# Expert layer: 160 instead of 128 tokens served by gathered rows, and 352 instead of 384 dense columns

## The reference, cut to what matters

```python
qh = (x2 @ w_q).reshape(t, PEER_HEADS, 2, PEER_QDIM // 2)
scores = jnp.einsum('thcd,hckd->thck', qh, sub_keys, ...)
sv, si = lax.top_k(scores, PEER_TOPK)
...
act = jax.nn.gelu(jnp.einsum('tkd,td->tk', expert_u[eb], xb, ...))
return jnp.einsum('tk,tkd->td', act * gb, expert_v[eb].astype(jnp.float32))
```

## Time and profile before

| What | Value |
|---|---|
| median of three runs | 4141.18 us (4139.8 to 4145.25) |
| the profiled execution's own time | 4136.7 us |
| its span in the trace | 4134.9 us |
| TensorE matmul busy | 3976.7 us, 96% |
| VectorE busy | 2549.7 us, 62% |
| ScalarE busy | 1551.5 us, 38% |
| GpSimd busy | 557.1 us, 13% |
| mean granted TensorE clock | 0.985 |

### The profile page before, as it was taken

The page is one execution under the profiler, slowest core; times in us unless marked ns, Lnnn a source line. Parts: engine busy times, 40 slices in busy tenths (PEclk is TensorE's granted clock), DMA queues, the critical chain, the costliest instruction groups (busy, mean ns, idle before and its releaser), DMA issues. The chain is left out here.

```text
span 4134.9 us, 50381 instructions
## 1 busy us (share of the span) xinstructions
PE 3976.7 (96%) x20625; PEld 3464.8 (84%) x20625; DVE 2549.7 (62%) x3795; ACT 1551.5 (38%) x2168; POOL 557.1 (13%) x405
## 2 busy tenths in 40 slices
PE   8999897999999899999999999999999999999998
PEld 7778797779999899999997887688888887678887
DVE  6432675679897876777776533775444442766443
ACT  3222124423666674333333224543222233744222
POOL 1000001010123333333322100100001110001000
PEclk9999999999999999999999999999999999999999
DMA  3344005333679889899983444142233434242222
GB/s 130 113 133 155 21 7 179 114 112 134 223 270 331 304 314 336 340 351 347 358 304 124 140 130 123 54 147 97 94 100 107 135 123 142 61 143 97 99 95 82
DMA packets 269057, 689.73 MB, mean 167 GB/s; under 512 B 19187, under 2 KB 52339, under 8 KB 251932
## 3 DMA queue, kind: packets, MB, share of 16 engines
q1 hardware_dynamic: 222748, 527.11, 37.1%
q0 software_dynamic: 36864, 134.23, 9.3%
q10 hardware_dynamic: 9216, 25.17, 1.5%
HBM read 585.50 MB, written 100.96 MB: 166 GB/s over the span
## 5 line engine op out<-in xcount | busy, mean ns | idle before, releaser
L1252 ACT CAST pe_w_high<-pe_w_raw 128x2048 fp32r<-128x2048 f32 (+1 forms) x168 | 317.0, 1887 | 524.3 <-DMA pe_w_raw<-in_peer_v_units 249.8
L1344 DVE TENSOR_TENSOR pe_w_low<-pe_w_raw,pe_w_high 128x2048 fp32r<-128x2048 f32 (+1 forms) x168 | 382.1, 2275 | 176.6 <-ACT pe_w_high L1252 174.7
L1139 PE MATMUL ps<-xn_p_high,pe_w_high 128*128 128x384 f32 (+1 forms) x1088 | 381.3, 350 | 34.2 <-DVE pe_w_low L1344 20.3
L2245 ACT CAST tail_w_high<-tail_w_raw 128x2048 fp32r<-128x2048 f32 (+3 forms) x124 | 221.8, 1794 | 442.5 <-DMA tail_w_raw<-in_w_in 144.3
L2254 DVE TENSOR_TENSOR tail_w_low<-tail_w_raw,tail_w_high 128x2048 fp32r<-128x2048 f32 (+3 forms) x124 | 265.7, 2147 | 186.4 <-ACT tail_w_high L2245 186.2
L1139 PE MATMUL ps<-xn_p_high,pe_w_low 128*128 128x384 f32 (+1 forms) x1088 | 371.4, 341 | 0.0
L1139 PE MATMUL ps<-xn_p_low,pe_w_high 128*128 128x384 f32 (+1 forms) x1088 | 371.2, 341 | 0.0
L1169 PE MATMUL ps<-pe_far_hidden_high,pe_w_high 128*128 128x384 f32 x1024 | 344.1, 336 | 9.3 <-DVE pe_near_hl L1470 4.7
L1169 PE MATMUL ps<-pe_near_hl,pe_w_high 128*128 128x384 f32 x1024 | 342.9, 335 | 0.0
L1169 PE MATMUL ps<-pe_far_hidden_high,pe_w_low 128*128 128x384 f32 x1024 | 342.8, 335 | 0.0
L1557 POOL DMA_INDIRECT home_pe_row<-in_peer_u,pe_expert x128 | 178.7, 1396 | 574.7 <-DVE pe_act L1530 377.6
(11 more groups left out here) (655 smaller groups left out, 9443.4 us busy)
## 6 DMA issues: line engine op xcount, KB each, us to landing
pe_w_raw<-in_peer_u_units SPq DMA_DIRECT2D x64, 1024.0 KB
pe_w_raw<-in_peer_v_units SPq DMA_DIRECT2D x64, 1024.0 KB
in_w_raw<-in_w_in SPq DMA_DIRECT2D x34, 1024.0 KB, 5.4
tail_w_raw<-in_w_up SPq DMA_DIRECT2D x32, 1024.0 KB, 5.5
tail_w_raw<-in_w_down SPq DMA_DIRECT2D x32, 1024.0 KB, 5.1
pe_w_raw<-in_w_in SPq DMA_DIRECT2D x28, 1024.0 KB
tail_w_raw<-in_w_in SPq DMA_DIRECT2D x28, 1024.0 KB, 5.1
dram_peer_hidden<-pe_rings_r ACTq DMA_DIRECT2D x64, 384.0 KB
```

The source lines that it names most:

```text
L1139: last = pe.matmul(ps[:, q, 0:n], w[:, s, at], xp[:, 4 * i + c, 0:n], start=(i == 0 and c == 0 and p == 0), stop=(i == 1 and c == 3 and p ...
L1252: act.copy(ring.flat(hi, u), ring.flat(raw, u)).then_inc(w_hi, 1)
L1344: dve.tensor_tensor(ring.flat(lo, u), ring.flat(raw, u), ring.flat(hi, u).bitcast(F32), ALU.subtract).then_inc(w_lo, 1)
L2245: act.copy(hi, raw).then_inc(self.w_hi, 1)
```

## The change

Thirty-two further tokens leave the dense way. Their 128 slots each are laid on four groups of 32 partitions (token t in group o holds slots 32o to 32o+31), so that 32 further gathers of u and 32 of v serve them: 160 + 160 gathers instead of 128 + 128. The dense way has 352 columns. The list of the 32 tokens is put on its partition groups by eight small DMAs on SyncE's queue, and their x is turned in a second tile `x_late`, four copies side by side. The last burst of gates has 32 tokens. The planner's `unit` follows from the columns (7.70 us), and sums are due from 55 us ahead of the down units instead of 5 us behind their start. The core of the diff, the repeated renamings left out:

```diff
-N_SPARSE = 128
-N_DENSE = T - N_SPARSE
-PASSES = PH * TOPK * N_SPARSE // P
+N_LATE = 32
+N_DENSE = T - P - N_LATE
+COPIES = P // N_LATE
+FIRST_PASSES = PH * TOPK
+PASSES = FIRST_PASSES + FIRST_PASSES // COPIES
...
-    GATE = lambda it: PICK[0] + 38.0 + (start(D0) - 25.0 - PICK[0] - 38.0 - 18.0 * (n_gates // 8)) / n_gates * it + 18.0 * (it // 8)
+    GATE = lambda it: PICK[0] + 38.0 + (start(D0) - 25.0 - PICK[0] - 38.0 - 18.0 * n_bursts) / n_gates * it + 18.0 * (it // 8)
...
-    first_dot, first_sum = PICK[3] + 55.0, start(D0) + 5.0
+    first_dot, first_sum = PICK[3] + 55.0, start(D0) - 55.0
+    LATE = PICK[2] + 75.0
...
                 def list_moves():
-                    if N_SPARSE < P:
-                        yield PICK[3] + 36.0
-                        sp.wait_ge(listed, 2)
-                        for t in (expert, share):
-                            sp.dma_start(t[0:N_SPARSE, 0:PASSES], t[N_SPARSE:P, PASSES:2 * PASSES]).then_inc(moved, 16)
+                    yield LATE
+                    sp.wait_ge(late_listed, 1)
+                    sp.wait_ge(ready, NT)
+                    per = FIRST_PASSES // COPIES
+                    for to, from_ in ((expert, digit), (share, ej)):
+                        rows_ = from_.rearrange("p h j -> p (h j)")
+                        for o in range(COPIES):
+                            sp.dma_start(to[o * N_LATE:(o + 1) * N_LATE, FIRST_PASSES:PASSES],
+                                         rows_[P - N_LATE:P, o * per:(o + 1) * per]).then_inc(late_moved, 16)
...
-                            parts = P // N_SPARSE
-                            for o in range(parts):
-                                last = pe.matmul(ps[:, n, N_DENSE:T], acc[:, n * P:(n + 1) * P], k.ident[:, o * N_SPARSE:(o + 1) * N_SPARSE],
-                                                 start=(o == 0), stop=(o == parts - 1))
+                            dims = slice(n * P, (n + 1) * P)
+                            for o in range(COPIES):
+                                pe.matmul(ps[:, n, N_DENSE:T - P], x_late[:, dims], k.ident[:, o * N_LATE:(o + 1) * N_LATE],
+                                          start=(o == 0), stop=(o == COPIES - 1))
+                            last = pe.matmul(ps[:, n, T - P:T], x_tok[:, dims], k.ident[:, :], start=True, stop=True)
...
+                        if m == 2:
+
+                            v(dve.tensor_scalar(digf, i1, float(NKEY), None, ALU.mult))
+                            v(dve.tensor_tensor(digf, digf, i2, ALU.add))
+                            dve.tensor_copy(digit, digf).then_inc(late_listed, 1)
...
-                            dve.tensor_tensor(to, to, by, ALU.mult).then_inc(h_scaled, 1)
...
+                            dve.tensor_tensor(to_whole, to_whole, by_whole, ALU.mult)
+                            dve.tensor_tensor(to[:, :, whole:N_DENSE], to[:, :, whole:N_DENSE], by_rest, ALU.mult).then_inc(h_scaled, 1)
...
+                    late = lambda a: a.unsqueeze(1).to_broadcast([P, COPIES, N_LATE])
+                    for c in range(NC_D):
+                        dve.scalar_tensor_tensor(x_two[1][:, c, :].rearrange("p (o t) -> p o t", o=COPIES), late(k.resid[:, c, N_DENSE:T - P]),
+                                                 gain[:, c:c + 1], late(rstd[:, N_DENSE:T - P]), ALU.mult, ALU.mult).then_inc(x_joined, 1)
...
+                            dve.wait_ge(late_moved, 32 * COPIES)
...
+                        if n == FIRST_PASSES:
+                            pool.wait_ge(late_moved, 32 * COPIES)
```

More of the change, by code:

```diff
@@ L952, in peer @@
     n_gates = N_DENSE // UNIT
+    n_bursts = -(-N_DENSE // BURST)
+    burst = lambda b: min(BURST, N_DENSE - BURST * b)
     def start(u):
@@ L992, in peer @@
     x_joined, x_turned, x_kept = sem("x_joined"), sem("x_turned"), sem("x_kept")
-    listed, moved, row_used, act_raised, folded = (sem(n) for n in ("listed", "moved", "row_used", "act_raised", "folded"))
+    late_listed, late_moved = sem("late_listed"), sem("late_moved")
+    listed, row_used, act_raised, folded = (sem(n) for n in ("listed", "row_used", "act_raised", "folded"))
     row_in = [k.gather_sem(f"{name}_row_in{s}") for s in range(DEPTH)]
@@ L1003, in peer @@
         r = rings.at("r", 0, [P, 3, 2 * N_DENSE])
[L1004 to L1007, removed]
+        x_two = [rings.at(f"x_two{i}", NC_D * P * i, [P, NC_D, P]) for i in range(2)]
+        x_tok, x_late = sb("x_tok", [P, D]), sb("x_late", [P, D])
+        of_pass = lambda j: x_tok if j < FIRST_PASSES else x_late
+        expert, share, act_s = sb("expert", [P, PASSES], U32), sb("share", [P, PASSES]), sb("act", [P, PASSES])
         rows = [k.home.at(f"{name}_row{s}", s * D, [P, D])[:, :] for s in range(DEPTH)]
@@ L1013, in peer @@
         rest = near.at("rest", 10240, [P, SETS, NKEY])
-        gate_out = near.at("gate_out", 0, [P, NKEY, BURST])
+        gate_out = [near.at(f"gate_out{t}", 0, [P, NKEY, t]) for t in (BURST, burst(n_bursts - 1))]
+        gates_of = lambda b: gate_out[0 if burst(b) == BURST else 1]
         J, I_ = ([near.at(f"{n}{s}", 8192 + 2048 * s + o, [P, UNIT, P])[:, :, :] for s in range(RING)] for n, o in (("J", 0), ("I", 1024)))
@@ L1069, in table_stores @@
                 def table_stores():
-                    for b in range(N_DENSE // BURST):
+                    for b in range(n_bursts):
                         for part in range(STORES):
-                            yield GATE(8 * b + 7) + 22.0 + unit * part
-                            sp.wait_ge(gate_kept, 16 * (b + 1))
+                            yield GATE(min(8 * b + 7, n_gates - 1)) + 22.0 + unit * part
+                            sp.wait_ge(gate_kept, min(16 * (b + 1), 2 * n_gates))
                             n = NKEY // STORES
                             quads = slice(part * n // QUAD, (part + 1) * n // QUAD)
-                            sp.dma_start(table.rearrange("u p (b x) -> p u b x", x=QUAD * BURST)[:, quads, b, :],
-                                         gate_out[:, part * n:(part + 1) * n, :].rearrange("p (u i) t -> p u (i t)", i=QUAD)
+                            columns = slice(QUAD * BURST * b, QUAD * (BURST * b + burst(b)))
+                            sp.dma_start(table.rearrange("u p x -> p u x")[:, quads, columns],
+                                         gates_of(b)[:, part * n:(part + 1) * n, :].rearrange("p (u i) t -> p u (i t)", i=QUAD)
                                          ).then_inc(gate_stored, 16)
@@ L1188, in x_turns @@
                     yield 9.0
-                    pe.wait_ge(x_joined, NC_D)
-                    for c in range(NC_D):
-                        last = pe.transpose(ps[:, 4 + c // 4, (c % 4) * P:(c % 4 + 1) * P], x_two[:, c, :], k.ident[:, :])
+                    pe.wait_ge(x_joined, 2 * NC_D)
+                    for i in range(2):
+                        for c in range(NC_D):
+                            last = pe.transpose(ps[:, 4 + 2 * i + c // 4, (c % 4) * P:(c % 4 + 1) * P], x_two[i][:, c, :], k.ident[:, :])
                     last.then_inc(x_turned, 1)
@@ L1318, in x_copies @@
                     act.wait_ge(x_turned, 1)
-                    for c in range(2):
-                        act.copy(x_tok[:, c * T:(c + 1) * T], ps[:, 4 + c, :]).then_inc(x_kept, 1)
+                    for i, to in enumerate((x_tok, x_late)):
+                        for c in range(2):
+                            act.copy(to[:, c * T:(c + 1) * T], ps[:, 4 + 2 * i + c, :]).then_inc(x_kept, 1)
                 def raise_sparse():
```

38 lines of the change are left out of this document (20 added, 18 removed).

## The result

The changed kernel takes 4164.38 us (median of 8 runs, the lowest 4151.01) beside 4145.01 us for the kernel before (8 runs): ratio 1.0042, 95% interval 1.003 to 1.0055. The change makes the kernel 0.4% slower, 19 us. I had forecast 4114 us, 27 us less than the three runs that I had then. One of the eight runs of the changed kernel took 7623 us, in a slower state; the ratio leaves it out, and the median of the other seven is 4163.55 us.

The account below looks back on a forecast made before the run. No single engine was taken as the bound: TensorE paced the down units, VectorE the choices, with DMA near full. Terms +3 + 4.5 + 12 - 23 - 22 = -26 us gave 4111 us, predicted median 4114 us, range 4078 to 4152.

Parts of the forecast that it names:

- What a unit costs TensorE: All 128 units: a matmul with 352 columns takes 0.160 us, a unit 7.67 us instead of 8.32.
- Start of the layer: Opening 106 us: eight more products and transposes ahead of TensorE's first units, +3 us.
- choices: VectorE-paced 118 us stretch: one more low half and two more dots, +4.5 us.
- the first half of the gates: 257 us stretch: added dots and low halves fill VectorE beyond the planned length, 269 us, +12.
- Second half of the gates: 304 us stretch: 104.4 MB moved at a DMA rate of 372 GB/s, 281 us, -23.
- Down units: 543 us stretch: at 372 GB/s a unit takes 8.1 us, 521 us in all, -22.
- The last unit: End of the down units: small identity products of 32 columns add 4 us.
- The sum: Whole kernel: the stretches' terms total -26 us, 4111 us profiled, 4114 us predicted for the median.
- SyncE's wait for the list: SyncE's queue: a weight load behind the wait may come late once, 0 to 10 us, taken at 0.
- the slow one: Rival: DMA engines already at their limit, 350 GB/s; kernel 21 us slower, 4163 us; chance 0.26 with its milder half.

Follow-up runs that it names:

- e2: Changed kernel with all gathers kept, but VectorE working on 8 instead of 1024 columns in every fifth slot; 4149 us, ratio 1.0012 to before.
- e1: Changed kernel with every fifth of the 320 gathers left out, VectorE's work on those slots kept; 4130 us, ratio 0.9963 to before.
- e5: Changed kernel with sums due 5 us behind the start of the down units instead of 55 us ahead; 4161 us, ratio 1.0036 to before.
- e6: Kernel before with sums due 55 us ahead of the down units, so its 128 dots are packed tighter; 4152 us, ratio 1.0014 to before.
- e8: Changed kernel with only VectorE's order in the down units altered, both low halves made earlier; 4131 us, ratio 0.9964 to before.
- e11: Changed kernel with new VectorE order in down units, sums due 5 us behind their start, SyncE's list step due 110 instead of 75 us; 4135 us.

## Why the prediction was wrong, step by step

**What a unit costs TensorE**: right, 0.159 against 0.160 us.

**Start of the layer, +3, choices, +4.5 us, and the first half of the gates, +12**: right in sign, 19.5 forecast and 25 measured. TensorE's query units end 0.3 us later, the first gate row starts at 1077.8 us instead of 1073.5, and the 192nd at 1323.9 instead of 1299.2. So the start and the choices cost 4 us instead of 7.5, and the first half 20 instead of 12. VectorE's busy time from 950 to 1325 is 347 us against 328. The reason I gave, VectorE full, is half of it: e2 shortens the up part by only 12 us. The other half is VectorE standing still for gathers, which I had not considered, though four buffers and the length of an issue were at hand.

**Second half of the gates, "104.4 / 0.372 = 281 us, -23"**: wrong. From the 192nd gate row to the down units it is 327.5 us, 330.2 before: about -3. The step took the DMA rate as what sets the length. e1, with fewer bytes, had only 10 us less up part, at 306 instead of 332 GB/s, so the rate was a result. The dots' packing, worth 12 us (e5, e6), was in my text as a formula for counting dots and not as a cost.

**Down units, "At 372 a unit takes 8.1 us ... 521 us, -22"**: wrong, 556 us, 8.7 us a unit. This is the step that turned the sign. The rate itself was well chosen: e8 reaches 365 GB/s and 517 us, within 4 us of the step's answer. What the step left out is that a rate is reached only if somebody asks in time. I wrote that the waits "eat the slack in a full queue", and never added up the chain: 10.9 us from issue to landing and 6.6 us of VectorE's order against two units of 7.67. VectorE's part of it stood in the earlier trace rows; of the landing had only the waits for it.

**The clock**: a term that is missing. With 556 us = 491 of matmuls, some 6 more of the last unit, 38 idle and up to 22 of lower clock, the down units add up. In the up part the mean of 0.95, 0.92 against 1.00, 0.98 is worth up to some 30 us. No term of my sum has the clock, though the earlier trace rows shows it.

**The last unit, 4 us**: it takes longer than that, the identity products run over 15.2 us instead of 9.1 (their first and last start):

```profile
L1187 PE MATMUL ps<-ident_sb,pe_x_late x64: 191/276/276, 2193.7 to 2208.9; 128*128 128x32 f32 x64
```

But what follows is 8 us shorter (1955 against 1963 us to the end of the span); the residual's additions overlap with the longer unit, so I take most of it as given back, without a run that shows it.

**The sum**: by the same steps the measured one is +4 (start and choices) + 20 - 3 + 14, and 8 less behind the layer: some 28 us more of span, where I had 26 less. The recorded sum has a slip of its own: 4111 + 4.5 is 4115.5 us, not 4114.

**SyncE's wait for the list**: it came (12.6 us), outside the 10 us of my bound, and cost nothing measurable (e11).

**The rivals**: the slow one named 4163 us, and 4164 was measured, but for the wrong reason. It has the DMA engines at their limit at 350 GB/s and TensorE waiting for low halves behind late loads; they ran at 338 with TensorE waiting in the down units for the low part of the hidden values alone, and gave 365 when VectorE's order was changed. The 358 GB/s of the Trainium skill's page "SBUF — State Buffer", section "Summary: rules for kernel authors", would have given the time before by the working in the prediction, and is not what held the kernel. The range's upper end, 4152, took in only half of that rival's loss; both kinds of loss that came, stalls behind VectorE and behind loads, were costs without a bound from above in my sum.

## What to carry to other kernels

Before a busy engine is made faster, add up the longest chain that must fit in its ring (issue, landing, each consumer in its fixed order) and compare it with the new length of the ring, and do the same for every other ring whose rate rises. Take late landings for this and not the median: here the median load fitted and the slower ones did not. If the chain no longer fits, the saving turns into waits, and in this kernel the longer waits also lowered TensorE's clock. The order of the instructions in a stream is then worth more than the work in it: one pair of due times gave 33 us in the changed kernel and 14 in the one before, where the whole change gave none.

## What the runs showed of the hardware that I had not expected

A matmul of 64 columns with fp32r operands, 0.213 us at a clock of 0.50, is slower than one of 352 at full clock (0.159 us); with TensorE busy throughout, the clock stayed at the lower level for more than 500 us. The loads of its weights were busy throughout as well, 0.333 us each instead of 0.188, so they may be what sets this step. Only this one kernel, run once, shows it, and whether the width alone is the reason stays open. The landing of a 512 KB gather grew from a median of 6.7 to 7.8 us between a DMA share near 0.85 and one of 0.9, small beside what it did to a ring that was just long enough.
